# A decoder step's last four experts: where the final norm's weights are loaded, how the down weights are cut, and where the final norm stands

## The chip, the cores and the metric

The kernel runs on one core of one Trainium2 chip. The metric is the device time of one launch in microseconds (us), from several runs of the same program; beside it stands one execution that the hardware profiler recorded. TensorE (PE in the profile) does the matmuls, VectorE (DVE) and ScalarE (ACT) the elementwise work, and SyncE (SP) issues almost all transfers. All data are 32-bit floats.

## The reference

One step of a hybrid decoder layer over 320 tokens (256 prompt positions and 8 groups of 8 sampled positions), width 2048. After the mixing part and a residual add, each token goes to 2 of 32 experts, and one last norm closes the step:

```python
def _rmsnorm(x, g):
    xf = x.astype(jnp.float32)
    y = xf * lax.rsqrt(jnp.mean(xf * xf, axis=-1, keepdims=True) + NORM_EPS)
    return (y * g.astype(jnp.float32)).astype(x.dtype)
...
def expert_block(args):
    xblk, e = args
    return (jax.nn.silu(xblk @ w_gate[e]) * (xblk @ w_up[e])) @ w_down[e]
...
x = x + _hier_moe(_rmsnorm(x, norm_ffn_g), router_coarse, router_fine,
                  exp_w_gate, exp_w_up, exp_w_down)
y_prompt = _rmsnorm(hp, norm_final_g)
y_sample = _rmsnorm(hs, norm_final_g)
```

Gate and up weights of one expert are 2048 x 512, down weights 512 x 2048: 4 MB each.

## The kernel before

The program has three stages: the projections and the two head groups, the output projection with the router, and the experts. Each engine has its own instruction stream, written out by hand, and semaphores order them; nothing is scheduled by a planner. The change lies in the last part of the experts' stage, and in what follows it.

**Experts.** They are worked on four at a time (`QUAD`), in eight turns (`EQ`). Each of the four has 32 token slots (`CAP`), so four small matmuls fill the array's columns side by side; a source matmul shows as two records in the profile. If an expert gets more than 32 tokens, the whole stage is repeated in another round (`ROUNDS`); `nround` holds the number of rounds, is read by every engine after the first round, and is 1 for these inputs. A turn takes 24 pieces of weights of 2 MB (`PIECES`): pieces 0 to 15 are gate and up, 16 to 23 are down. They go into eight slots of SBUF (`NSLOT_C`, filled in the order `ESLOT`). SP asks for a piece as soon as `ex_used` says that the piece eight before it has been used; `ex_in[slot]` counts arrivals.

**The last turn** (`ex_last_quad`, and the branch `last_quad` in PE's `experts`) treats the down weights differently from the turns before: the output's 2048 columns are done in four blocks of `F` = 512 (n = 0 to 3), each in a PSUM bank of its own (`DB`: ps_C, ps_SB, ps_YB, ps_RT). Two pieces belong to a block, 16 + 2n and 17 + 2n; a piece holds two experts' columns of the block with all 512 rows. When a block's 16 matmuls (32 records, L983) are done, ACT copies the bank to `yp`, PE multiplies by the gates' transpose `gT` for the three token tiles (`combine`, L921, 6 records; tiles of 128, 128 and 64 tokens, `TT_`), and DVE adds each result to `acc` (`combined`). Every DVE and ACT operation is recorded under the line of a helper (L1286 and L1027). ACT squares and sums each part of `acc`. For blocks 0 to 2 DVE also multiplies `acc` by the final norm's weights into `og`.

**The final norm's weights** (`gfin`, spread over 128 partitions, 1 MB, into `gfb`, the place of the gathered tokens `xg`) are the last thing that SP asks for in this turn. DVE waits for them ahead of block 0's `combined`:

```python
dve.wait_ge(gfin_in, 16 * (rd + 1))
for m in range(NB):
    combined(m, True)
    if m < NB - 1:
        for t, (t0, nt) in enumerate(TT_):
            c = slice(m * F, (m + 1) * F)
            last = TT(og[0:nt, t, c], acc[0:nt, t, c], gfb[0:nt, c], ALU.mult)
```

`combine` uses two PSUM banks in turn (ps_PJ), so PE can be at most two products ahead of DVE.

**The close** stands behind the place where each engine reads `nround` and branches over the further rounds: DVE sums the squares (TENSOR_REDUCE), ACT takes the root, DVE the reciprocal, then DVE and ACT scale the rows, and SP stores them in six transfers to `o_y` (2.62 MB in all).

Of the kernel before, what the change touches and what calls it, by code (L numbers as in the profile page):

```python
# [6 lines left out]
ALU = mybir.AluOpType  # L7
# [93 lines left out]
def build_program(nc, xT, win, w_out, params, lora_mu, shT, lora_w, gmix, cst, head_cst,  # L101
# [3 lines left out]
    with ctx:  # L105
# [106 lines left out]
        over, cmx = sb(ROUNDS - 1), sb(1)  # L212
# [20 lines left out]
        og = arena[:, og_at:og_at + 9 * F].rearrange("p (t n) -> p t n", t=3)  # L233
# [109 lines left out]
        r_in, gfin_in, out_y = sem("router_in"), sem("gfin_in"), sem("out_y")  # L343
# [37 lines left out]
        def _(sp):  # L381
# [135 lines left out]
            def ex_last_quad(it):  # L517
                for c in range(PIECES):
                    sp.wait_ge(ex_used, PIECES * it + c - NSLOT_C + 1)
                    if c < 4 * QUAD:  # L520
                        ex_piece(EQ - 1, c, it)
                    else:
                        s = ESLOT[c % NSLOT_C]
                        n, e = (c - 4 * QUAD) // 2, NE - QUAD + c % 2 * 2
                        dst = arena[:, experts_at + s * BIGSLOT:experts_at + (s + 1) * BIGSLOT].rearrange("p (h k n) -> p h k n", h=2, k=4)
                        src = w_down[e:e + 2, :, n * F:(n + 1) * F].rearrange("h (k p) n -> p h k n", k=4)
                        sp.dma_start(dst, src).then_inc(ex_in[s], 16)
                sp.wait_ge(ex_used, PIECES * it + 4 * QUAD)
                sp.dma_start(gfb, gfin).then_inc(gfin_in, 16)
# [16 lines left out]
            ex_last_quad(EQ - 1)  # L546
            sp.wait_ge(named["routed"], 1)
            r = sp.value_load(nround[0:1, 0:1], min_val=1, max_val=ROUNDS)
            with sp.If(r > 1):
                with sp.Fori(1, r) as rd:  # L550
                    sp.wait_ge(named["og_done"], rd)
                    sp.nop().then_inc(sem("round_loads"), 1)
                    with sp.Fori(0, EQ - 1) as i:
                        ex_quad(i, EQ * rd + i)
                    ex_last_quad(EQ * rd + EQ - 1)
                sp.nop()
# [3 lines left out]
            def rows(t):  # L560
                t0, nt = TT_[t]
                return o_y[t0:t0 + nt, :]

            for i, t in enumerate((0, 1, 2)):
                sp.wait_ge(named["fin_done"], i + 1)
                sp.dma_start(rows(t)[:, 3 * F:], acc[0:TT_[t][1], t, 3 * F:]).then_inc(out_y, 16)
                if i == 0:
                    sp.wait_ge(named["fin_scaled"], 1)
                    sp.dma_start(rows(0)[:, 0:3 * F], og[:, 0, :]).then_inc(out_y, 16)
            sp.wait_ge(named["fin_done"], 4)  # L570
            sp.dma_start(rows(1)[:, 0:3 * F], og[:, 1, :]).then_inc(out_y, 16)
            sp.wait_ge(named["fin_scaled"], 2)
            sp.dma_start(rows(2)[:, 0:3 * F], og[0:TT_[2][1], 2, :]).then_inc(out_y, 16)
# [8 lines left out]
        def _(pe):  # L582
# [345 lines left out]
            def experts(it, opening, more, before, again, rd=None):  # L928
# [93 lines left out]
        def _(act):  # L1022
# [195 lines left out]
            def experts(it, opening, more, before, again, rd=None):  # L1218
# [9 lines left out]
                if rd is not None:  # L1228
                    for m in range(NB):
# [5 lines left out]
                    act.nop().then_inc(named["d_free"], 1)  # L1235
                    return
# [31 lines left out]

            act.nop().then_inc(named["squares_done"], 1)
            act.wait_ge(named["sum_of_squares"], 1)  # L1270
            A(rstd, ss, ACT.Sqrt, bias=eps[:, 0:1], scale=1.0 / D).then_inc(named["fin_root"], 1)
# [667 lines left out]
```

## Time and profile before

| | us |
|---|---|
| median of three runs | 2056.57 |
| lowest and highest | 2054.83, 2058.86 |
| the profiled execution | 2057.36 |
| its span, first to last instruction | 2055.6 |
| PE busy | 1678.6 (82%) |
| DVE busy | 604.0 (29%) |
| ACT busy | 280.3 (14%) |

A span is 1.8 us less than the time of the same execution. Shares of busy time are means over stages with different limits, so they don't say what the end of the program waits for. Times in the rows below count from the start of the span.

### The profile page before, as it was taken

Reading aid. Unit: us, or ns where it says so; the run is one execution under the profiler, and the core shown is the slowest. Engines: PE = TensorE matmul, PEld = TensorE weight load, DVE = VectorE, ACT = ScalarE, POOL = GpSimd, SP = SyncE. Lnnn points to the kernel's source line nnn. Section 1 sums busy time; section 2 is a strip of 40 time slices with the busy share of each in tenths; the row PEclk is TensorE's granted clock in tenths of the full one; section 3 lists DMA queues with packets and bytes.
Section 4 is the critical chain, followed back from the end, with each engine's and each line's share of the span. In section 5 each row is a group of like instructions: output and inputs, shape, how many; then the busy total and the mean of one; then the engine's idle time right before and its main releaser. Section 6 shows DMA issues by size and latency. Waiting matters only on the chain.

```text
span 2055.6 us, 25652 instructions
## 1 busy us (share of the span) xinstructions
PE 1678.6 (82%) x9134; PEld 1019.9 (50%) x9134; DVE 604.0 (29%) x1092; ACT 280.3 (14%) x559; POOL 123.9 (6%) x101
## 2 busy tenths in 40 slices
PE   8998999999999989899999577675867858576554
PEld 4776767677767767676675223132322313232111
DVE  6536263545444453631012101111110101010013
ACT  2221212222121212120012000000000000000002
POOL 0201111110202020200000000000000000000000
PEclk9999999999999999999999878887888878788777
DMA  7223222322122222316526999999999999999992
GB/s 277 98 76 111 76 89 75 110 68 97 65 91 92 74 89 75 110 49 242 216 112 290 427 427 428 428 429 429 429 428 429 429 429 429 428 429 429 428 394 103
DMA packets 71039, 510.34 MB, mean 248 GB/s; under 512 B 20400, under 2 KB 23600, under 8 KB 37584
## 3 DMA queue, kind: packets, MB, share of 16 engines
q1 hardware_dynamic: 70944, 509.60, 61.5%
q8 instruction: 29, 0.48, 0.1%
q14 instruction: 18, 0.15, 0.0%
q0 software_dynamic: 48, 0.12, 0.0%
HBM read 499.87 MB, written 9.82 MB: 248 GB/s over the span
## 4 chain that ended last, share of the span: by engine, by line
PE 52%; DMA 32%; DVE 10%; issue 2%; SPq 2%; ACT 1%; DVEq 1%; ACTq 0%
DMA arena<-w_up 21%; PE ps_PJ L626 16%; DVE arena L1286 10%; DMA arena<-w_down 10%; PE ps_C L945 8%; PE ps_PJ L824 6%; PE ps_C L684 2%; PE ps_C L707 1%; SPq L510 1%; ACT arena L1027 1%; PE ps_C L995 1%; PE ps_SB L995 1%; DMA arena<-gfin 1%; PE ps_YB L995 1%; PE ps_RT L790 1%
## 5 line engine op out<-in xcount | busy, mean ns | idle before, releaser
L626 PE MATMUL ps_PJ<-arena 128*128 128x320 f32 x1792 | 542.2, 434 | 4.0 <-ACTq L374 4.0
L945 PE MATMUL ps_C<-arena 128*32 128x512 f32 x2048 | 282.2, 714 | 179.7 <-DMA arena<-w_gate 97.3
L626 PEld LDWEIGHTS ps_PJ<-arena 128*128 128x128 f32 x1792 | 319.8, 190 | 111.5 <-issue 11.6
L945 PEld LDWEIGHTS ps_C<-arena 128*32 128x32 f32 x2048 | 80.1, 128 | 375.7 <-issue 373.5
L1286 DVE TENSOR_TENSOR arena<-arena,ps_PJ 128x512 f32<-128x512 f32 (+2 forms) x112 | 73.5, 656 | 592.3 <-PE ps_PJ L921 433.3
L1027 ACT ACTIVATE arena<-ps_C 128x512 f32<-128x512 f32 (+1 forms) x68 | 40.7, 598 | 1068.1 <-PE ps_C L945 594.6
L1286 DVE TENSOR_TENSOR arena<-arena 128x320 f32<-128x320 f32 (+12 forms) x236 | 160.0, 678 | 46.9 <-ACTq L374 26.0
L1756 POOL TENSOR_TENSOR arena<-arena 128x640 f32<-128x640 f32 (+2 forms) x80 | 118.2, 1477 | 780.6 <-DVEq L374 423.1
L824 PE MATMUL ps_PJ<-arena 128*128 128x320 f32 x512 | 145.8, 437 | 2.1 <-DVEq L374 2.1
L914 PE MATMUL ps_PJ<-arena 128*128 128x128 f32 (+1 forms) x768 | 136.2, 308 | 0.0
L914 PEld LDWEIGHTS ps_PJ<-arena 128*128 128x128 f32 (+1 forms) x768 | 104.4, 188 | 40.8 <-issue 11.7
L921 PE MATMUL ps_PJ<-arena 128*128 128x512 f32 (+1 forms) x192 | 97.1, 626 | 26.7 <-DVEq L374 23.2
L1286 DVE TENSOR_TENSOR arena<-ps_PJ,arena 128x512 f32<-128x512 f32 x32 | 22.1, 692 | 323.1 <-PE ps_PJ L914 322.9
L824 PEld LDWEIGHTS ps_PJ<-arena 128*128 128x128 f32 x512 | 95.8, 192 | 41.3 <-issue 6.4
L1027 ACT ACTIVATE arena<-arena 128x320 f32<-128x320 f32 (+11 forms) x148 | 79.7, 538 | 175.6 <-DVEq L374 89.0
L1286 DVE COPY arena<-ps_C 128x128 f32<-128x128 f32 (+2 forms) x98 | 41.6, 424 | 168.5 <-PE ps_C L716 104.8
L995 PE MATMUL ps_C<-arena 128*32 128x512 f32 x224 | 41.5, 821 | 60.6 <-DMA arena<-w_down 58.4
L921 PEld LDWEIGHTS ps_PJ<-arena 128*128 128x128 f32 (+1 forms) x192 | 26.7, 171 | 95.8 <-DVEq L374 68.5
L1286 DVE SCALAR_TENSOR_TENSOR arena<-arena 128x320 f32<-128x320 f32 (+5 forms) x146 | 68.3, 468 | 13.8 <-DVE arena L1286 8.8
L1286 DVE TENSOR_TENSOR arena<-arena,ps_C 128x512 f32<-128x512 f32 x56 | 38.6, 689 | 111.2 <-PE ps_C L707 108.9
L1027 ACT ACTIVATE arena<-ps_PJ 128x256 f32<-128x256 f32 (+2 forms) x96 | 37.0, 385 | 232.5 <-PE ps_PJ L626 142.3
L1286 DVE RECIPROCAL arena<-arena 128x320 f32<-128x320 f32 (+1 forms) x29 | 54.6, 1881 | 17.2 <-ACTq L374 14.5
(183 smaller groups left out, 1363.5 us busy)
## 6 DMA issues: line engine op xcount, KB each, us to landing
arena<-w_gate SPq DMA_DIRECT2D x64, 2048.0 KB, 20.2
arena<-w_up SPq DMA_DIRECT2D x64, 2048.0 KB, 21.0
arena<-w_down SPq DMA_DIRECT2D x64, 2048.0 KB, 21.1
arena<-win SPq DMA_DIRECT2D x59, 1024.0 KB, 4.8
arena<-w_out SPq DMA_DIRECT2D x16, 1024.0 KB, 6.7
arena<-xT SPq DMA_DIRECT2D x8, 640.0 KB, 6.9
arena<-s_ret SPq DMA_DIRECT2D x8, 512.0 KB, 3.8
o_sret<-arena SPq DMA_DIRECT2D x8, 512.0 KB, 3.8
```

The lines of the kernel that those rows point to most:

```text
L510: sp.dma_start(dst, src).then_inc(ex_in[s], 16)
L626: last = mm(pj(j)[:, 0:T], wt[j % NSLOT][:, kt, :], hT[:, kt, :], start=kt == 0, stop=kt == KT - 1)
L684: last = mm(b[:, i * P:(i + 1) * P], Lm[:, k % 2, c, :], V[:, c, :], start=True, stop=True)
L707: last = mm(bank("dv" + k)[:, c * P:(c + 1) * P], U[:, c, :], Z[:, c, :], start=True, stop=True)
L824: last = mm(pj(m)[:, 0:T], w[:, i, :], yT[:, KORD[i], :], start=i == 0, stop=i == KT - 1)
L914: last = mm(XB[b][:, k * P:(k + 1) * P], x1[0:nt, t, kt * P:(kt + 1) * P], pick[0:nt, t, :], start=t == 0, stop=t == 2)
L921: mm(XB[b][0:nt, :], gT[:, t0:t0 + nt], yp[:, n * F:(n + 1) * F], start=True, stop=True).then_inc(x_full[b], 1)
L945: last = mm((GB, UB)[u][h * CAP:(h + 1) * CAP, :], xg[:, kt, h * CAP:(h + 1) * CAP], w[h][:, k, :], start=kt == 0, stop=kt == KT - 1)
L995: last = mm(DB[n][h * CAP:(h + 1) * CAP, :], hhT[:, 2 * k + j, h * CAP:(h + 1) * CAP], w[h][:, j, n * F:(n + 1) * F], start=k + j == 0, st ...
L1027: ins = nc.scalar.activation(*args, **kw)
L1286: ins = build(*args)
L1756: ins = nc.gpsimd.tensor_tensor(*args)
```

## The change

There are three parts.

1. SP asks for `gfin` behind piece 19, in front of pieces 20 to 23, and DVE waits for it behind block 0's `combined`.
2. A piece of down weights of the last turn now holds half the rows of all four experts (`e` is the half), where it held all rows of two. PE waits for a block's second piece in the middle of the block.
3. The close stands inside the round, in front of the reading of `nround`. ACT does a square root of one element that nobody reads (`unread`) behind the transposed gates' copy; the last block's product with the weights is split off for two tiles, and rows are scaled and stored in other pieces.

```diff
@@ -521,12 +521,38 @@
                         ex_piece(EQ - 1, c, it)
...
-                        n, e = (c - 4 * QUAD) // 2, NE - QUAD + c % 2 * 2
-                        dst = arena[:, experts_at + s * BIGSLOT:experts_at + (s + 1) * BIGSLOT].rearrange("p (h k n) -> p h k n", h=2, k=4)
-                        src = w_down[e:e + 2, :, n * F:(n + 1) * F].rearrange("h (k p) n -> p h k n", k=4)
+                        n, e = (c - 4 * QUAD) // 2, c % 2
+                        dst = arena[:, experts_at + s * BIGSLOT:experts_at + (s + 1) * BIGSLOT].rearrange("p (h k n) -> p h k n", h=4, k=2)
+                        src = w_down[NE - QUAD:NE, :, n * F:(n + 1) * F].rearrange("h (k e p) n -> e p h k n", k=2, e=2)[e, :, :, :, :]
                         sp.dma_start(dst, src).then_inc(ex_in[s], 16)
-                sp.wait_ge(ex_used, PIECES * it + 4 * QUAD)
-                sp.dma_start(gfb, gfin).then_inc(gfin_in, 16)
+                    if c == 4 * QUAD + 3:
+                        sp.wait_ge(ex_used, PIECES * it + 4 * QUAD)
+                        sp.dma_start(gfb, gfin).then_inc(gfin_in, 16)
...
+                sp.wait_ge(named["fin_done"], 4 * rd + 1)
+                sp.nop().then_inc(sem("stores_begun"), 1)
+                sp.dma_start(rows(0, 0, 2 * F), og[:, 0, 0:2 * F]).then_inc(stored, 16)
+                sp.wait_ge(named["fin_scaled"], 2 * rd + 1)
+                sp.nop().then_inc(sem("stores_begun"), 1)
+                sp.dma_start(rows(1, 2 * F, D), og[:, 1, 2 * F:]).then_inc(stored, 16)
...
+            store_rows(0, out_y)
             sp.wait_ge(named["routed"], 1)
             r = sp.value_load(nround[0:1, 0:1], min_val=1, max_val=ROUNDS)
...
-            def rows(t):
-                t0, nt = TT_[t]
-                return o_y[t0:t0 + nt, :]
-
-            for i, t in enumerate((0, 1, 2)):
-                sp.wait_ge(named["fin_done"], i + 1)
-                sp.dma_start(rows(t)[:, 3 * F:], acc[0:TT_[t][1], t, 3 * F:]).then_inc(out_y, 16)
-                if i == 0:
-                    sp.wait_ge(named["fin_scaled"], 1)
-                    sp.dma_start(rows(0)[:, 0:3 * F], og[:, 0, :]).then_inc(out_y, 16)
-            sp.wait_ge(named["fin_done"], 4)
-            sp.dma_start(rows(1)[:, 0:3 * F], og[:, 1, :]).then_inc(out_y, 16)
-            sp.wait_ge(named["fin_scaled"], 2)
-            sp.dma_start(rows(2)[:, 0:3 * F], og[0:TT_[2][1], 2, :]).then_inc(out_y, 16)
...
                 if last_quad:
                     pe.wait_ge(named["gT_done"], it + 1)
                     for n in range(NB):
-                        w = [piece_in(4 * QUAD + 2 * n + e, it).rearrange("p (h k n) -> p h k n", h=2, k=4) for e in range(2)]
                         for k in range(4):
+                            if k % 2 == 0:
+                                w = piece_in(4 * QUAD + 2 * n + k // 2, it).rearrange("p (h k n) -> p h k n", h=4, k=2)
                             for h in range(QUAD):
-                                last = mm(DB[n][h * CAP:(h + 1) * CAP, :], hhT[:, k, h * CAP:(h + 1) * CAP], w[h // 2][:, h % 2, k, :],
+                                last = mm(DB[n][h * CAP:(h + 1) * CAP, :], hhT[:, 2 * (k % 2) + k // 2, h * CAP:(h + 1) * CAP], w[:, h, k % 2, :],
                                           start=k == 0, stop=k == 3)
-                                if k == 3 and h % 2 == 1:
-                                    last.then_inc(ex_used, 1)
+                            if k % 2 == 1:
+                                last.then_inc(ex_used, 1)
                         pe.wait_ge(named["yp_part"], NB * rd + n + 1)
                         combine(n)
...
                 if rd is not None:
+                    A(unread, eps[:, 0:1], ACT.Sqrt)
                     for m in range(NB):
                         act.wait_ge(ex_used, PIECES * it + 4 * QUAD + 2 * m + 2)
                         A(yp[:, m * F:(m + 1) * F], DB[m][:, :], ACT.Copy).then_inc(named["yp_part"], 1)
...
+                    act.nop().then_inc(named["squares_done"], 1)
+                    act.wait_ge(named["sum_of_squares"], rd + 1)
+                    A(rfin, ss, ACT.Sqrt, bias=eps[:, 0:1], scale=1.0 / D).then_inc(named["fin_root"], 1)
+                    act.wait_ge(named["acc_done"], rd + 1)
+                    A(og[:, 1, 2 * F:], og[:, 1, 2 * F:], ACT.Copy, scale=rfin[:, 1:2]).then_inc(named["fin_scaled"], 1)
+                    nt = TT_[2][1]
+                    A(og[0:nt, 2, 0:3 * F], og[0:nt, 2, 0:3 * F], ACT.Copy, scale=rfin[0:nt, 2:3]).then_inc(named["fin_scaled"], 1)
...
-                dve.wait_ge(gfin_in, 16 * (rd + 1))
-                for m in range(NB):
+
+                def gained(m, t):
+                    nt = TT_[t][1]
+                    c = slice(m * F, (m + 1) * F)
+                    TT(og[0:nt, t, c], acc[0:nt, t, c], gfb[0:nt, c], ALU.mult)
+
+                for m in range(NB - 1):
                     combined(m, True)
-                    if m < NB - 1:
-                        for t, (t0, nt) in enumerate(TT_):
-                            c = slice(m * F, (m + 1) * F)
-                            last = TT(og[0:nt, t, c], acc[0:nt, t, c], gfb[0:nt, c], ALU.mult)
-                last.then_inc(named["og_done"], 1)
+                    if m == 0:
+                        dve.wait_ge(gfin_in, 16 * (rd + 1))
+                    for t in range(3):
+                        gained(m, t)
+                combined(NB - 1, True)
+                gained(NB - 1, 0)
+                dve.wait_ge(named["squares_done"], rd + 1)
+                RED(ss, ss4[:, :, :], AX_X, ALU.add).then_inc(named["sum_of_squares"], 1)
+                gained(NB - 1, 1)
+                dve.wait_ge(named["fin_root"], rd + 1)
+                RECIP(rfin, rfin).then_inc(named["acc_done"], 1)
+                TSC(og[:, 0, 0:2 * F], og[:, 0, 0:2 * F], rfin[:, 0:1], None, ALU.mult).then_inc(named["fin_done"], 1)
+                TSC(og[:, 0, 2 * F:], og[:, 0, 2 * F:], rfin[:, 0:1], None, ALU.mult).then_inc(named["fin_done"], 1)
+                TSC(og[:, 1, 0:2 * F], og[:, 1, 0:2 * F], rfin[:, 1:2], None, ALU.mult).then_inc(named["fin_done"], 1)
+                nt = TT_[2][1]
+                STT(og[0:nt, 2, 3 * F:], acc[0:nt, 2, 3 * F:], rfin[0:nt, 2:3], gfb[0:nt, 3 * F:], ALU.mult, ALU.mult).then_inc(named["fin_done"], 1)
...
-            dve.wait_ge(named["squares_done"], 1)
-            RED(ss, ss4[:, :, :], AX_X, ALU.add).then_inc(named["sum_of_squares"], 1)
-            dve.wait_ge(named["fin_root"], 1)
-            RECIP(rstd, rstd).then_inc(named["acc_done"], 1)
-            for t, (t0, nt) in enumerate(TT_):
-                a_ = acc[0:nt, t, 3 * F:]
-                STT(a_, a_, rstd[0:nt, t:t + 1], gfb[0:nt, 3 * F:], ALU.mult, ALU.mult).then_inc(named["fin_done"], 1)
-            TSC(og[:, 1, :], og[:, 1, :], rstd[:, 1:2], None, ALU.mult).then_inc(named["fin_done"], 1)
```

What is left out: the other four stores are written like the two that stand (tile 0 columns 1024 on behind `fin_done` 2, tile 1 columns 0 to 1024 behind `fin_done` 3, tile 2 columns 1536 on behind `fin_done` 4, tile 2 columns 0 to 1536 behind `fin_scaled` 2), `og` grows from 4608 to 6144 words, the old close on ACT is taken out like the one on DVE, and further rounds, which do not happen here, get the same treatment.

On SP's queue, the end of the first round, from the last turn's gate and up pieces on. First before, then changed:

```order
L510 DMA arena<-w_gate 128x4096 x4
L510 DMA arena<-w_up 128x4096 x4
L527 DMA arena<-w_down 128x8x512 x8
L529 DMA arena<-gfin 128x2048
L548 TENSOR_LOAD nround
L548 ISA x2
L549 COMPARE_AND_BRANCH
```

```order
L527 DMA arena<-w_down 128x8x512 x4
L530 DMA arena<-gfin 128x2048
L527 DMA arena<-w_down 128x8x512 x4
L540 DMA o_y<-arena 128x1024
L543 DMA o_y<-arena 128x1024
L546 DMA o_y<-arena 128x1024
L549 DMA o_y<-arena 128x1024
L552 DMA o_y<-arena 64x512
L555 DMA o_y<-arena 64x1536
L575 TENSOR_LOAD nround
```

The weights' transfer has moved past four pieces, and the stores past the reading of `nround` and its branch.

On PE, block 3 of the last turn with the semaphores that its first instructions wait for (the rows of the other blocks are alike). First before, then changed:

```order
L983 MATMUL ps_RT<-arena 32x512 [waits expert_in3,expert_in2]
L983 MATMUL ps_RT<-arena 32x512 x15
L921 MATMUL ps_PJ<-arena 128x512 [waits x_free1,yp_part]
L921 MATMUL ps_PJ<-arena 128x512 [waits x_free0]
L921 MATMUL ps_PJ<-arena 64x512 [waits x_free1]
```

```order
L999 MATMUL ps_RT<-arena 32x512 [waits expert_in2]
L999 MATMUL ps_RT<-arena 32x512 x7
L999 MATMUL ps_RT<-arena 32x512 [waits expert_in3]
L999 MATMUL ps_RT<-arena 32x512 x7
L936 MATMUL ps_PJ<-arena 128x512 [waits x_free1,yp_part]
```

The number of matmuls is the same; the wait for the second piece has moved eight matmuls back.

On DVE, from block 3's sums to the scaled rows. Before, the first three rows stand at the end of the round, and the others behind the code of the further rounds:

```order
L1286 TENSOR_TENSOR arena<-arena,ps_PJ 128x512 x2
L1286 TENSOR_TENSOR arena<-arena,ps_PJ 64x512
L1732 TENSOR_LOAD nround
...
L1733 UNCONDITIONAL_BRANCH
L1737 UNCONDITIONAL_BRANCH
L1286 TENSOR_REDUCE arena<-arena 128x3
L1289 ISA
L1286 RECIPROCAL arena<-arena 128x3
```

```order
L1302 TENSOR_TENSOR arena<-arena,ps_PJ 128x512 x2
L1302 TENSOR_TENSOR arena<-arena,ps_PJ 64x512
L1302 TENSOR_TENSOR arena<-arena 128x512
L1302 TENSOR_REDUCE arena<-arena 128x3
L1302 TENSOR_TENSOR arena<-arena 128x512
L1302 RECIPROCAL arena<-arena 128x3
L1302 TENSOR_SCALAR arena<-arena 128x1024 x3
L1302 SCALAR_TENSOR_TENSOR arena<-arena 64x512
L1764 TENSOR_LOAD nround
```

Between the last sum and the reduction the load and the branches are gone and one product has come in; a second stands between the reduction and the reciprocal.

## Rows read from the trace of the kernel before

**Rows 1.** Part 2 of the page: transfers' busy share in tenths, 40 slices.

```profile
DMA  7223222322122222316526999999999999999992
```

**Rows 2.** Busy time in stretches: PE, PEld, DVE, ACT, POOL; granted clock, DMA share, GB/s.

```profile
1940.00:1962.00 22.00, 14.09 (x75) 4.03 (x75) 2.74 (x4) 0.00 (x0) 0.00 (x0) 0.72 1.01 429
1966.00:2010.00 44.00, 18.94 (x107) 6.10 (x107) 1.80 (x3) 2.23 (x4) 0.00 (x0) 0.66 1.05 387
2047.00:2055.00 8.00, 0.00 (x0) 0.00 (x0) 1.76 (x2) 1.40 (x1) 0.00 (x0) 0.50 0.95 323
```

**Rows 3.** SP's issues of pieces 20 and 23; below each its time to landing.

```profile
1977.16 2.77 SPq L527 DMA_DIRECT2D arena<-w_down  x1
...
arena<-w_down SPq DMA_DIRECT2D x1, 2048.0 KB, 17.5
...
1991.31 5.29 SPq L527 DMA_DIRECT2D arena<-w_down  x1
...
arena<-w_down SPq DMA_DIRECT2D x1, 2048.0 KB, 19.5
```

**Rows 4.** The chain that ended last, from 1980 on: start, us, what.

```profile
1982.64 5.54 PE ps_C L983 x32
...
1996.65 16.61 DMA arena<-gfin
...
2013.29 0.70 DVE arena L1286
```

**Rows 5.** Timeline of PE, 1976 to 2042: start, us, operation, idle before.

```profile
1980.01 1.11 PE L966 MATMUL ps_PJ<-arena 128*128 128x128 f32 x4 [2.86 <-DVEq L374]
...
1988.90 1.98 PE L921 MATMUL ps_PJ<-arena 128*128 128x512 f32 x4 [0.78 <-ACTq L374]
...
2014.09 1.97 PE L921 MATMUL ps_PJ<-arena 128*64 128x512 f32 x2 [23.20 <-DVEq L374]
...
2028.54 3.11 PE L921 MATMUL ps_PJ<-arena 128*128 128x512 f32 x6 [0.85 <-ACTq L374]
2031.58 3.64 PE L983 MATMUL ps_RT<-arena 128*32 128x512 f32 x32
2036.07 3.11 PE L921 MATMUL ps_PJ<-arena 128*128 128x512 f32 x6 [0.85 <-ACTq L374]
```

**Rows 6.** Timeline of all engines, 2013 to 2056.

```profile
2032.62 2.14 DVE L1286 TENSOR_TENSOR arena<-arena 128x512 f32<-128x512 f32 x3 [0.25 <-DVE arena L1286]
...
2035.38 0.60 ACT L1027 ACTIVATE arena<-ps_RT 128x512 f32<-128x512 f32 x1 [2.03 <-PE ps_RT L983]
...
2040.68 0.19 ACT L1027 ACTIVATION_READ_ACCUMULATOR arena<-arena 64x1 f32 x1
2042.31 1.28 ACT L1027 ACT_TABLE_LOAD   x1 [1.44 <-issue]
2044.23 0.17 DVE L1286 TENSOR_REDUCE arena<-arena 128x3 f32<-128x12 f32 x1 [4.33 <-issue]
...
2044.87 0.18 DVE L1286 RECIPROCAL arena<-arena 128x3 f32<-128x3 f32 x1 [0.47 <-ACTq L374]
...
2046.04 0.37 SPq L566 DMA_DIRECT2D o_y<-arena  x1
...
2047.90 1.02 DVE L1286 TENSOR_SCALAR arena<-arena 128x1536 f32<-128x1536 f32 x1
```

**Rows 7.** Transfers from 2040 to 2044.5 by kind.

```profile
q8 instruction: 2, 0.03, 3.3%
q14 instruction: 2, 0.02, 1.4%
```

**Rows 8.** Stretches as in rows 2: around the first and the second restart of PE.

```profile
1976.90:1980.00 3.10, 0.25 (x4) 0.00 (x0) 1.80 (x3) 0.60 (x1) 0.00 (x0) 0.93 1.05 386
...
1983.00:1986.40 3.40, 3.40 (x20) 0.92 (x16) 0.00 (x0) 0.00 (x0) 0.00 (x0) 0.50 1.05 387
...
2017.00:2041.00 24.00, 19.46 (x114) 5.12 (x106) 12.36 (x18) 9.03 (x23) 0.00 (x0) 1.00 0.01 2
```

More of the change, by code:

```diff
@@ L211, in build_program @@
         oh1, oh2 = (sb(3 * EG).rearrange("p (t n) -> p t n", t=3) for _ in range(2))
-        over, cmx = sb(ROUNDS - 1), sb(1)
+        over, cmx, unread, rfin = sb(ROUNDS - 1), sb(1), sb(1), sb(3)
         assert place[0] <= top[0], (place[0], top[0])
@@ L232, in build_program @@
         og_at = experts_at + ESLOT[0] * BIGSLOT
-        og = arena[:, og_at:og_at + 9 * F].rearrange("p (t n) -> p t n", t=3)
+        og = arena[:, og_at:og_at + 3 * D].rearrange("p (t n) -> p t n", t=3)
         SETUP = [(0, 2), (2, 2), (4, 4), (8, 4), (12, 4)]
@@ L342, in build_program @@
         x_in, x1T_done, tr_full, tr_free = [sem(f"x_in{i}") for i in range(4)], sem("x1T_done"), sem("transposed"), sem("x1_done")
-        r_in, gfin_in, out_y = sem("router_in"), sem("gfin_in"), sem("out_y")
+        r_in, gfin_in, out_y, out_more = sem("router_in"), sem("gfin_in"), sem("out_y"), sem("out_more")
         x_full, x_free = [sem("x_full0"), sem("x_full1")], [sem("x_free0"), sem("x_free1")]
@@ new lines, in rows, with store_rows @@
+            def rows(t, a, b):
+                t0, nt = TT_[t]
+                return o_y[t0:t0 + nt, a:b]
+            def store_rows(rd, stored):
+                sp.wait_ge(named["fin_done"], 4 * rd + 1)
[4 more added lines that the diff above has]
+                sp.dma_start(rows(1, 2 * F, D), og[:, 1, 2 * F:]).then_inc(stored, 16)
+                sp.wait_ge(named["fin_done"], 4 * rd + 2)
+                sp.nop().then_inc(sem("stores_begun"), 1)
+                sp.dma_start(rows(0, 2 * F, D), og[:, 0, 2 * F:]).then_inc(stored, 16)
+                sp.wait_ge(named["fin_done"], 4 * rd + 3)
+                sp.nop().then_inc(sem("stores_begun"), 1)
+                sp.dma_start(rows(1, 0, 2 * F), og[:, 1, 0:2 * F]).then_inc(stored, 16)
+                sp.wait_ge(named["fin_done"], 4 * rd + 4)
+                sp.nop().then_inc(sem("stores_begun"), 1)
+                sp.dma_start(rows(2, 3 * F, D), og[0:NS * TS, 2, 3 * F:]).then_inc(stored, 16)
+                sp.wait_ge(named["fin_scaled"], 2 * rd + 2)
+                sp.nop().then_inc(sem("stores_begun"), 1)
+                sp.dma_start(rows(2, 0, 3 * F), og[0:NS * TS, 2, 0:3 * F]).then_inc(stored, 16)
@@ L550, in _ @@
                 with sp.Fori(1, r) as rd:
-                    sp.wait_ge(named["og_done"], rd)
-                    sp.nop().then_inc(sem("round_loads"), 1)
+                    sp.wait_ge(out_y, 96)
                     with sp.Fori(0, EQ - 1) as i:
@@ L555, in _ @@
                     ex_last_quad(EQ * rd + EQ - 1)
+                    store_rows(rd, out_more)
+                    sp.wait_ge(out_more, 96 * rd)
+                    sp.nop().then_inc(sem("stores_begun"), 1)
                 sp.nop()
@@ L1267, in _ @@
             n[0], n[1] = base + per * r, 0
-            act.nop().then_inc(named["squares_done"], 1)
-            act.wait_ge(named["sum_of_squares"], 1)
-            A(rstd, ss, ACT.Sqrt, bias=eps[:, 0:1], scale=1.0 / D).then_inc(named["fin_root"], 1)
-            act.wait_ge(named["acc_done"], 1)
-            for t in (0, 2):
-                nt = TT_[t][1]
-                A(og[0:nt, t, :], og[0:nt, t, :], ACT.Copy, scale=rstd[0:nt, t:t + 1]).then_inc(named["fin_scaled"], 1)
         @block.vector
```

## The prediction

> **What bounds the kernel now.** I read the page's slices first. From the 21st slice on the transfers are busy nine tenths or more in every slice but the last [rows 1]: the experts' stage is set by the weights' stream, and PE, granted 0.72 of its full clock, waits for it. The stretches give the rate: 429 GB/s for gate and up pieces, 387 GB/s for the last turn's down pieces, which are cut into runs of 2 KB [rows 2]. So a 2 MB down piece (2,097,152 bytes) takes 5.4 us, a block's two pieces 10.8 us, and gfin's 1 MB about 2.4 us. No transfer in this stage is removed or added, so the stream ends when it ended. What can change is how much work stands behind its end.
>
> Then the chain. Block 0's matmuls run from 1982.64, and then nothing until gfin lands: 1996.65 + 16.61 = 2013.26, and DVE's first sum starts at 2013.29 [rows 4]. The last down piece had landed at 1991.31 + 19.5 = 2010.8 [rows 3]. PE had made block 0's first two products at 1988.90 (4 records) and then stood for 23.2 us, since DVE had freed neither bank [rows 5]. So almost four blocks' sums, three blocks' matmuls, the close and the stores all lie behind the stream: 2055.6 - 2013.3 = 42.3 us. I make the sum against the span of 2055.6; the same execution's time is 2057.36, the median of the runs 2056.57, and I take the gain in the span off the median.
>
> **Parts 1 and 2: gfin earlier, pieces by halves of the rows.** Up to piece 19 nothing changes. SP now waits for all 16 gate and up pieces before gfin, where piece 20 needed 13; these four are released within the last four matmuls of one group, so that wait ends together with the old one, at 1977.16 [rows 3]. The queue runs 17.5 to 19.5 us ahead of the landing [rows 3], so the longer issue of 5.3 us starves nothing. Pieces 20 to 23 land 2.4 us later each: 20 at 1977.16 + 17.5 + 2.4 = 1997.1, then one per 5.4 us at 2002.5, 2007.9 and 2013.3. gfin lands 2.4 us behind piece 19, which lands 5.4 before 1994.7: at 1991.7.
>
> Block 0 is summed when its products come. At the full clock, 3.04 us lie between a block's first product and the next block's matmuls (2028.54 to 2031.58) and 4.49 us between those and the block's own first product (2031.58 to 2036.07) [rows 5]. From 1988.90: block 1's matmuls start at 1991.9, after its pieces; block 2's at 1999.5, waiting from 2001.3 to 2002.5 for piece 21; its products start at 2005.2, block 3's matmuls at 2008.2, after piece 22. Half of them are done at 2010.1, and PE waits 3.2 us for piece 23. DVE's gfin wait sits behind the first three sums, past 1991.7: hidden; if gfin came later, 4 us are free before block 1's sums need DVE.
>
> What stays behind the last piece, at the full clock:
> - half a block's matmuls: 3.64 / 2 = 1.8 us, and 0.85 through ACT's copy to the first product (2035.22 to 2036.07) [rows 5, 6];
> - from the first product to the end of the last square's readout: 2036.07 to 2040.87, 4.8 us [rows 5, 6].
>
> That puts the last square's end at 2013.3 + 7.5 = 2020.8.
>
> **Part 3: the close in the round.** Before, the reduction started at 2044.23, 3.36 us after that square, with nothing in front of it but the load of `nround` and the branches (4.33 us idle, "issue"); four instruction fetches run in that stretch [rows 6, 7]. That goes. In its place come two products of 128x512, 2.14 / 3 = 0.71 us each with 0.25 between operations [rows 6]. The first stands beside the last square and is hidden. The second stands between the reduction and the reciprocal. I allow 0.1 us from the square to the reduction, then 0.17 + 0.25 + 0.71 + 0.2 = 1.35 to the reciprocal, where it was 0.64. The table load of 1.28 us [rows 6], hidden behind DVE's stall before, would stand on this path now, but the root that nobody reads takes it to about 1982.4, before ACT's first copy, which waits for matmuls until 1988; without that cover it would cost about 1.3. The reciprocal starts at 2020.8 + 1.45 = 2022.25, where it was 2044.87.
>
> The stores: before, the first was issued 1.17 us behind the reciprocal's start, and the span ended at +10.7; the stream of 2.62 MB was the limit, 323 GB/s at a busy share of 0.95 [rows 2, 6]. Now the first store is ready after one 128x1024 scaling (1.02 x 1024 / 1536 = 0.68 us [rows 6]), at +1.1, but with 512 KB where there were 256. ACT's two scalings lie beside DVE's. Bounds: +10.7 at the same rate, +9.4 if 2.62 MB move at 387 GB/s (6.8 us, not 8.1). I take +10.3, since the last transfer is still the one of 64 rows that used few runs. End: 2032.55.
>
> **The clock.** After 2.86 us without a matmul (up to 1980.01) the granted clock was 0.5, still so at 1986.4 though PE was back at work; while blocks followed each other with 0.85 us gaps it stayed at 1.0, from 2017 to 2041 [rows 5, 8]. The new wait for piece 23 is 3.2 us, so I expect the lower level (1.2 GHz) right where the rest of the path begins. The half block then takes 3.6, not 1.8; a product's two records took 1.97 at that level (2014.09) against about 1.1 [rows 5], which adds up to 2.2 over three products if the level lasts through them. So 1.5 to 4.0; I take 2.5, since the lower level lasted 2.9 us of work in one case (2014.09 to 2017) and at least 6.4 in the other (1980.01 to 1986.4). Gain: 2055.6 - 2035.05 = 20.5 us; 2056.57 - 20.5 = **2036.1**.
>
> The Trainium skill, TensorE: Matmul & The Clock Gate, section "HAM oscillation — how this bites in real kernels", says that bursts shorter than the wait for the next load are each run at the lower clock. The 2.86 us case agrees. It speaks against cutting a block in two around a wait: by the page the sum is 2036.1, and without its rule 2033.5, the first rival.
>
> **The rivals.**
> - *The clock holds over the last wait.* For it: the wait is shorter than most of those that lowered the clock, and any earlier delay of a block fills it. Then 2056.57 - 23.0 = 2033.5.
> - *PE, not the stream, paces the blocks.* At the lower level throughout, matmuls take 7.3, and the products up to 5.6 with 0.85 before them: 13.7 a block, against 10.8 of stream. Block 3 would start at 2019.4 and the reciprocal at 2036.5: span 2046.8, time 2047.8. Against it: the work from 1988.9 on is nearly continuous and such work held 1.0 [rows 8]. Half way, one block at the lower level, costs up to 2 us beyond 2033.5, since block 3 has 3.2 us to spare.
> - *SP ends last.* SP now reads `nround` and branches behind its last store, at about +4.9 (DVE's last scaling ends near +3.8, then two issues of 0.4 to 0.6 us); DVE's same passage took 4.33 us [rows 6]. That gives +9.2, hidden below +10.3; if the fetches queue behind the stores, up to 4 us more: 2037 to 2040. The Trainium skill, Runtime: NRT & Kernel Launch, section "Instruction fetch mechanics", says a taken branch out of the loaded pages stalls on a fetch; rows 7 agree.
> - *Slower than before: the new pieces read slowly.* A piece now takes rows of four experts instead of two. If the eight pieces went at 263 GB/s instead of 387, they would take 63.8 us instead of 43.4 and eat the 20.5. Below that rate it decides. Going from large runs to 2 KB runs cost only a tenth [rows 2], and runs and their number stay as they are. At 340 GB/s the time would be 2042.
> - *The order does not do what it says:* gfin, though asked for earlier, lands with the last piece. Then the blocks stand as before, and what is left is the stall of 3.4 less the product of 0.7, and 0.4 in the stores: 2053.5. Against it: landings kept the order of asking.
>
> **How the numbers follow.** The clock falls: 0.56. It holds: 0.2. PE paces, in part or whole (2037 to 2048): 0.08. SP ends last: 0.05. Pieces slower but still a gain (2038 to 2052): 0.06. gfin late: 0.01. No change from something unforeseen: 0.01. Slower than before: 0.03. So faster 0.95, the same 0.02, slower 0.03. A difference of 0.2% (4.1 us) is what a measurement of this kernel can tell. The first two cases, with stores +9.4 to +10.7 and a clock cost up to 4.0, span 2032.6 to 2038; to hold 8 in 10 with part of the others I give 2032.5 to 2041.
>
> **What would show it.** gfin lands near 1991.7 and the last down piece near 2013.3; DVE sums block 0 from 1990 on; PE stands some 3 us in the middle of block 3's matmuls, and the second half takes 3.6 us at a clock of 0.5; no "issue" wait in front of the reduction, and no table load there; reciprocal between 2022 and 2026, the end 9.4 to 10.7 us later. Wrong would make it: down pieces below 387 GB/s; a block whose matmuls start later than its second piece lands; an end that SP reaches well after the last store has landed.

## The result, and the profile after

The changed kernel takes 2036.76 us (median of four runs, 2034.52 to 2037.36), the kernel before in the same comparison 2056.41: ratio 0.9905, 95% interval 0.9892 to 0.9917. That is 19.7 us less; 20.5 were forecast. The profiled execution took 2036.68 us, with a span of 2034.9.

First SP's timeline in the changed kernel, as in [rows 3]: its issue of gfin (start, us) and of the four last pieces.

```profile
1975.49 2.27 SPq L530 DMA_DIRECT2D arena<-gfin  x1
1977.81 19.19 SPq L527 DMA_DIRECT2D arena<-w_down  x4
```

The same kernel's transfers, with the time from issue to landing at the end, which answers to [rows 4]:

```profile
arena<-gfin SPq DMA_DIRECT2D x1, 1024.0 KB, 14.2
```

gfin lands at 1975.5 + 14.2 = 1989.7. Then PE's timeline, which answers to [rows 5] (start, us, operation, records, idle before and who ended it).

```profile
1987.21 3.03 PE L936 MATMUL ps_PJ<-arena 128*128 128x512 f32 x6 [0.82 <-ACTq L374]
1990.18 3.64 PE L999 MATMUL ps_SB<-arena 128*32 128x512 f32 x32
...
2000.59 1.92 PE L999 MATMUL ps_YB<-arena 128*32 128x512 f32 x16 [0.98 <-DMA arena<-w_down]
...
2006.38 1.92 PE L999 MATMUL ps_RT<-arena 128*32 128x512 f32 x16
2011.22 2.94 PE L999 MATMUL ps_RT<-arena 128*32 128x512 f32 x16 [2.92 <-DMA arena<-w_down]
2014.96 4.83 PE L936 MATMUL ps_PJ<-arena 128*128 128x512 f32 x6 [0.80 <-ACTq L374]
```

Block 0's six product records run through at 1987.21, where PE stood for 23.2 us before; all that is left behind the last piece is half of block 3, which waited 2.92 us. That half took 2.94 us against 1.92 for the first, and the products 4.83 against 3.11 [rows 5]. The stretches say why (columns as in rows 2; the granted clock is the third number from the end):

```profile
2006.40:2012.00 5.60, 2.68 (x25) 0.68 (x28) 2.74 (x4) 1.45 (x4) 0.00 (x0) 1.00 0.47 176
2012.00:2018.80 6.80, 6.00 (x17) 1.51 (x10) 0.71 (x2) 1.32 (x3) 0.00 (x0) 0.50 0.00 0
```

PE ran at 2.4 GHz up to 2012.0 and at 1.2 GHz for the next 6.8 us. Next the changed kernel's timeline of the close, as in [rows 6]:

```profile
2021.30 0.19 ACT L1043 ACTIVATION_READ_ACCUMULATOR arena<-arena 64x1 f32 x1
2021.71 0.17 DVE L1302 TENSOR_REDUCE arena<-arena 128x3 f32<-128x12 f32 x1 [0.26 <-ACTq L1253]
...
2022.03 0.69 DVE L1302 TENSOR_TENSOR arena<-arena 128x512 f32<-128x512 f32 x1 [0.15 <-DVE arena L1302]
2022.75 0.18 DVE L1302 RECIPROCAL arena<-arena 128x3 f32<-128x3 f32 x1
...
2024.01 0.35 SPq L540 DMA_DIRECT2D o_y<-arena  x1
...
2028.29 1.21 SPq L555 DMA_DIRECT2D o_y<-arena  x1
```

SP's own instructions behind the stores, by source line (L575 loads `nround`, L576 branches, L592 holds the first instructions behind the branch, L105 is the end of the program; count, ns min/median/max, first and last start):

```profile
L575 SPq TENSOR_LOAD <-nround x1: 1577/1577/1577, 2029.5 to 2029.5; - x1
...
L576 SPq COMPARE_BRANCH  x1: 50/50/50, 2031.5 to 2031.5; - x1
...
L592 SPq EVENT_SEMAPHORE  x2: 17/22/28, 2034.3 to 2034.4; - x2
...
L105 SPq COMPARE_BRANCH  x1: 41/41/41, 2034.5 to 2034.5; - x1
```

And the last store among the transfers, with its time to landing:

```profile
o_y<-arena SPq DMA_DIRECT2D x1, 384.0 KB, 4.8
```

The "issue" wait of 4.33 us in front of the reduction is gone. But the last store, issued at 2028.29, landed 4.8 us later, at 2033.1, and SP got from its branch at 2031.5 to the end's first instruction only at 2034.5: the program ends 1.8 us behind the last landing. Before, that was 0.4 us (2049.75 + 5.4 = 2055.15, end 2055.58).

### The profile page after: what moved, and what is told of

Its sections match the earlier page's. It is cut to its first block, busy times and chain, and to the rows that moved or that the text cites. A ratio compares the mean times of both kernels' runs of the same rounds, so it can differ in the third digit from the quotient of the medians.

```text
span 2034.9 us, 25650 instructions
## 1 busy us (share of the span) xinstructions
PE 1682.4 (83%) x9134; PEld 1020.5 (50%) x9134; DVE 605.2 (30%) x1094; ACT 279.8 (14%) x560; POOL 124.0 (6%) x101
## 4 chain that ended last, share of the span: by engine, by line
PE 52%; DMA 32%; DVE 10%; issue 2%; SPq 1%; ACT 1%; DVEq 1%; ACTq 0%
DMA arena<-w_up 21%; PE ps_PJ L641 16%; DMA arena<-w_down 11%; DVE arena L1302 10%; PE ps_C L960 8%; PE ps_PJ L839 7%; PE ps_C L699 2%; PE ps_C L722 1%; SPq L510 1%; ACT arena L1043 1%; PE ps_C L1011 1%; PE ps_SB L1011 1%; PE ps_YB L1011 1%; PE ps_RT L805 1%; PE ps_SB L756 1%
## 5 line engine op out<-in xcount | busy, mean ns | idle before, releaser
L1302 DVE SCALAR_TENSOR_TENSOR arena<-arena 128x320 f32<-128x320 f32 (+4 forms) x144 | 66.8, 464 | 13.5 <-DVE arena L1302 8.7
## 6 DMA issues: line engine op xcount, KB each, us to landing
arena<-w_up SPq DMA_DIRECT2D x64, 2048.0 KB, 20.9
arena<-w_down SPq DMA_DIRECT2D x64, 2048.0 KB, 20.8
```

Of the source, the lines that this page charges most:

```text
L1302: ins = build(*args)
```

## The experiments

Executions differ by some 2 us either way before the part that changed is reached: PE got the last down piece at 2011.2 here and between 2009.4 and 2013.4 over the ten profiles with gfin early. In the kernel before, that piece landed at 2010.8, with gfin 2.4 behind it. So besides ratios I read each profile from the point where PE (or DVE) gets what it last waited for to the end of the span. I call it the **tail**. "Second half" and "products" are the last block's 16 records behind the wait and its six product records.

| kernel | last wait ends, us | tail, us | second half | products | time (median), us | ratio (95%) |
|---|---|---|---|---|---|---|
| before | 2013.29 (gfin) | 42.3 | | 3.11 | | 1 |
| changed | 2011.22 | 23.7 | 2.94 | 4.83 | 2036.76 | 0.9905 (0.9892 to 0.9917) |
| part 1 | 2009.40 | 23.9 | | 3.11 | 2036.85 | 0.9911 (0.9894 to 0.9927) |
| parts 1, 2 | 2011.15 | 22.0 | 1.92 | 3.11 | 2036.55 | 0.9909 (0.9893 to 0.9926) |
| part 2 | 2011.9 (gfin) | 42.5 | | 3.11 | 2055.77 | 1.0001 (0.9992 to 1.0011) |
| part 3 | 2011.4 (gfin) | 42.0 | | 3.11 | 2055.33 | 0.9995 (0.9986 to 1.0005) |
| parts 1, 3 | 2011.72 | 22.9 | | 3.11 | 2036.41 | 0.9905 (0.9888 to 0.9921) |

**Part 1 alone.**

```diff
+                    if c == 4 * QUAD + 3:
+                        sp.wait_ge(ex_used, PIECES * it + 4 * QUAD)
+                        sp.dma_start(gfb, gfin).then_inc(gfin_in, 16)
-                sp.wait_ge(ex_used, PIECES * it + 4 * QUAD)
-                sp.dma_start(gfb, gfin).then_inc(gfin_in, 16)
...
-                dve.wait_ge(gfin_in, 16 * (rd + 1))
                 for m in range(NB):
                     combined(m, True)
+                    if m == 0:
+                        dve.wait_ge(gfin_in, 16 * (rd + 1))
```

> The kernel before with part 1 alone: gfin asked for behind piece 19, DVE's wait for it behind block 0's sums; pieces and close as before. Theory A (the time is what stands behind the last down piece): three blocks' matmuls and the first three blocks' sums move under the stream, a whole block 3 (3.6 us, with the lower clock up to 6), its sums, the stall of 3.4 us and the close stay: about 15.5 us less than before, 2041 us. Rival B (most of the gain comes from the close, the landing order hardly counts): at most 4 us less, 2052 or more.

Measured 2036.85 us: as far as the times can tell, this part by itself is the whole gain. Rival B is out. Theory A's direction holds, but it took this version 4.2 us too slow. Part of the reason is in this kernel's PE timeline:

```profile
1998.84 6.26 PE L984 MATMUL ps_YB<-arena 128*32 128x512 f32 x32 [5.07 <-DMA arena<-w_down]
2005.95 3.11 PE L922 MATMUL ps_PJ<-arena 128*128 128x512 f32 x6 [0.84 <-ACTq L374]
2009.40 3.64 PE L984 MATMUL ps_RT<-arena 128*32 128x512 f32 x32 [0.34 <-DMA arena<-w_down]
```

With whole pieces PE waits 5.07 us for block 2, whose matmuls then run slowly (6.26 us), and that leaves only 0.34 us to wait before block 3, which runs at the full clock. The lower level was paid where there was time for it. The expectation had put it on block 3, at up to 2.4 us (6 for 3.6); where the rest of the 4.2 comes from is not shown. The tail is what the rows of the kernel before give at the full clock: from block 3's first matmul to its end it has 24.0 us (2031.58 to 2055.58), and here it is 23.9.

**Parts 1 and 2.** The edit is part 1's and the pieces' from the diff of the change.

> The kernel before with parts 1 and 2: gfin early and pieces by halves of the rows, the close as before. Theory A: half of block 3's matmuls move in front of the last landing, 1.8 us at the full clock and up to 3.6 at the lower one, less than with part 1 alone: 2038 to 2039.5 us. Rival C (the wait inside the block lowers the clock, which eats what the halves bring): equal to part 1 alone within 0.5 us.

The times don't tell it from part 1 (2036.55 against 2036.85, intervals overlap). The tails do: 22.0 against 23.9. PE waited 2.87 us inside block 3 and yet the clock held, so the half took 1.92. Theory A's 1.8 is measured at 1.9 in the tail for the case that the clock holds, but its 2038 to 2039.5 us was 1.5 to 3 us too slow, since it rests on the expectation for part 1. Rival C describes the other case, as the changed kernel's own profile shows.

**Part 2 alone.**

> The kernel before with part 2 alone: pieces by halves, gfin still last. Theory A: all pieces have landed when gfin does, so nothing changes: within 1 us of before, and the down stretch still moves 387 GB/s. Rival D (pieces that read from four experts are read at another rate): a rate other than 387 GB/s in that stretch, and the time moves by the stretch's difference.

Ratio 1.0001. The down stretch moves what it moved before [rows 2]; the stretch in this kernel:

```profile
1965.00:2008.00 43.00, 16.59 (x107) 5.13 (x107) 1.80 (x3) 2.23 (x4) 0.00 (x0) 0.75 1.05 388
```

388 GB/s against 387: how many experts a piece reads from makes no difference, and rival D is out.

**Part 3 alone.**

> The changed kernel with gfin last and its wait ahead of block 0's sums, and the old pieces: part 3 alone. Theory A: the stall of 3.4 us goes, a product of 0.7 stays in front of the reciprocal, and the stores with SP's load and branch behind them end 12.1 us behind it where it was 10.7, as in the changed kernel's trace: about 1.5 us less than before, 2055 us. Rival B: the close brings most of the 20 us: below 2045 us.

Ratio 0.9995, tail 42.0 against 42.3. The reduction came 0.2 us behind the last square instead of 3.4, the reciprocal 1.04 behind that instead of 0.64, and the end 12.05 behind the reciprocal (2041.40 to 2053.45) instead of 10.7. That is 1.4 us won, and in this execution block 1's matmuls took 5.30 us at the lower clock where they took 4.17 before, which hides 1.1 of it. From part 1 to parts 1 and 3 the tail shrinks by 1.0. The times show none of this: part 3 alone has an interval that includes 1, and the intervals of part 1 and of parts 1 and 3 overlap.

**Parts 1 and 3** (the changed kernel with whole pieces).

> The changed kernel with the old pieces (all rows of two experts): parts 1 and 3. Measured so far: part 1 alone has 24.1 us from the last down piece's landing to the end, with block 3 whole and at the full clock since PE waits only 0.3 us for it. Theory A: the halves take 1.9 us of matmuls off the path but put a wait of 2.9 us inside the block that lowers the clock; without them the path is 1.7 longer and the clock holds: from the landing to the end 23 to 24 us, within 1 us of the changed kernel (23.7). Rival: 1.8 to 2 us slower than the changed kernel.

Tail 22.9, time 2036.41: nothing is lost without the halves. In the changed kernel's profile they took 1.7 us of matmuls off the tail and put 2.7 back through the clock.

**gfin asked for last, DVE's wait still behind block 0's sums.**

```diff
-                    if c == 4 * QUAD + 3:
-                        sp.wait_ge(ex_used, PIECES * it + 4 * QUAD)
-                        sp.dma_start(gfb, gfin).then_inc(gfin_in, 16)
+                sp.wait_ge(ex_used, PIECES * it + 4 * QUAD)
+                sp.dma_start(gfb, gfin).then_inc(gfin_in, 16)
```

> The changed kernel with gfin asked for last again; DVE's wait stays behind block 0's sums. Theory A (the transfer's place counts, through DVE's sums and PE's two banks): block 1's sums wait for gfin, so one block less than before stands behind it: some 7.5 us less than with the close alone, 2047 us. Rival (the wait's place in DVE's stream is what counts): as fast as the changed kernel plus the 2.4 us of transfer, 2039 us.

2049.43 us, ratio 0.9967 (0.9955 to 0.998). PE is one block further when it stops. Its timeline in this kernel, and DVE's first work behind gfin:

```profile
1993.11 1.98 PE L935 MATMUL ps_PJ<-arena 128*128 128x512 f32 x4 [0.82 <-ACTq L374]
...
2011.32 2.14 DVE L1301 TENSOR_TENSOR arena<-arena 128x512 f32<-128x512 f32 x3 [21.88 <-DMA arena<-gfin]
...
2014.29 1.97 PE L935 MATMUL ps_PJ<-arena 128*64 128x512 f32 x2 [19.19 <-DVEq L374]
2016.19 5.76 PE L998 MATMUL ps_YB<-arena 128*32 128x512 f32 x32
```

So the chain runs through DVE's in-order stream and PE's two banks, and the place of the transfer counts; the rival's 2039 us is out. It is 2.4 us slower than expected. The tail is 37.2 us (2011.32 to 2048.5), 4.8 less than with the close alone, not 7.5. The expectation had left out that DVE, once gfin is there, first does block 0's three products (2.14 us) and only then the sum that frees PE's bank: PE restarts 3.0 us behind gfin, where it was 0.8 with the close alone. That is 2.2 of the 2.7 us. The rest is block 2's matmuls at the lower clock, 5.76 us, where the block behind gfin took 5.30 with the close alone.

**gfin early, DVE's wait in its old place.**

```diff
+                dve.wait_ge(gfin_in, 16 * (rd + 1))
                 for m in range(NB - 1):
                     combined(m, True)
-                    if m == 0:
-                        dve.wait_ge(gfin_in, 16 * (rd + 1))
```

> The changed kernel with DVE's wait for gfin in its old place, ahead of block 0's sums; gfin is still asked for early. Theory A: gfin lands 1.3 us behind block 0's first product, that delay fits into the waits for pieces 21 and 23, and nothing is left of it at the end: as the changed kernel within 0.5 us. Rival (the place of the wait matters): 1 us or more slower.

2034.22 us, ratio 0.9898 (0.9882 to 0.9915), tail 20.8. PE stood 0.88 us for block 0's third product, and nothing of it reached the end; moving DVE's wait brought nothing by itself. The tail is 2.9 us below the changed kernel's, which is what the lower clock cost there (2.7), since here the clock held over a wait of 2.63 us. Nothing more can be read from it.

**No square root that nobody reads.**

```diff
-                    A(unread, eps[:, 0:1], ACT.Sqrt)
```

> The changed kernel without the square root that nobody reads. The table load of 1.28 us then stands in front of ACT's root, behind the last square. Theory A: the root starts about 0.9 us later, of which the product beside it hides some: reciprocal 0.5 to 0.8 us later relative to the last square. Rival: 1.3 us later, the whole load.

The timeline of ACT and DVE in this kernel:

```profile
2022.09 0.19 ACT L1043 ACTIVATION_READ_ACCUMULATOR arena<-arena 64x1 f32 x1
2022.44 1.28 ACT L1043 ACT_TABLE_LOAD   x1 [0.17 <-ACT arena L1043]
...
2024.18 0.18 DVE L1301 RECIPROCAL arena<-arena 128x3 f32<-128x3 f32 x1 [0.68 <-ACTq L374]
```

From the last square's readout to the reciprocal 1.90 us (2022.28 to 2024.18) instead of 1.26 (2021.49 to 2022.75): 0.64, as theory A had it. The times can't show that: 2032.81 us, ratio 0.9887 (0.9871 to 0.9904), over runs from 2032.64 to 2038.17.

**SP's load of `nround` ahead of the stores**, the branch still behind them.

```diff
-            store_rows(0, out_y)
             sp.wait_ge(named["routed"], 1)
             r = sp.value_load(nround[0:1, 0:1], min_val=1, max_val=ROUNDS)
+            store_rows(0, out_y)
```

> The changed kernel with SP's load of nround in front of the stores' waits; the branch still stands behind them. Theory A (SP's load of 1.6 us and its branch of 2.8 us end the program, 1.2 us behind the last store's landing): the load's 1.6 us go from SP's path, and the end is set by the last store: 1.2 to 1.4 us less than the changed kernel. Rival (the last store's landing sets the end anyway): no difference.

Theory A fell. 2036.09 us, ratio 0.9902 (0.9885 to 0.9918), and what follows the branch did not start earlier, by SP's instructions in this kernel:

```profile
L576 SPq COMPARE_BRANCH  x1: 50/50/50, 2029.6 to 2029.6; - x1
...
L592 SPq EVENT_SEMAPHORE  x2: 17/22/28, 2034.2 to 2034.3; - x2
...
L105 SPq COMPARE_BRANCH  x1: 41/41/41, 2034.4 to 2034.4; - x1
```

It is 4.6 us from the branch to the instructions behind it (L592), where the changed kernel has 2.8, and 4.8 to the end's first instruction, where that has 3.0; SP ends at about the same distance behind the stores. What it waits for is not its own work, and it isn't the landing either: in the next run, whose branch comes first, L592 starts 3.4 us before the end's first instruction.

**Branch first.** Load and branch ahead of the stores, which then stand in both arms.

```diff
-            store_rows(0, out_y)
             sp.wait_ge(named["routed"], 1)
             r = sp.value_load(nround[0:1, 0:1], min_val=1, max_val=ROUNDS)
             with sp.If(r > 1):
+                store_rows(0, out_y)
...
             with sp.Else():
-                sp.nop()
+                store_rows(0, out_y)
```

> The changed kernel with SP's load of nround and its branch ahead of the stores, which stand in both arms. In the trace with the load alone moved, the branch took 4.6 us instead of 2.8 and ended at the same distance from the last store. Theory E (the branch's instruction fetches wait behind the stores' data in the same transfer engines): with the branch done before the first store, the program ends 0.4 us behind the last landing, as before: 1.0 to 1.3 us less than the changed kernel. Rival (something else at the end takes this time): no difference.

The same instructions in this kernel, where the branch is L575:

```profile
L575 SPq COMPARE_BRANCH  x1: 50/50/50, 1998.2 to 1998.2; - x1
...
L592 SPq EVENT_SEMAPHORE  x2: 17/22/28, 2029.9 to 2029.9; - x2
...
L105 SPq COMPARE_BRANCH  x1: 41/41/41, 2033.3 to 2033.3; - x1
```

From the reciprocal (2023.07) to the end (2033.7) it is 10.6 us, where the changed kernel has 12.15: 1.5 less, a little more than theory E's 1.0 to 1.3. In times 2034.54 us, ratio 0.9894 (0.9878 to 0.9911); the interval overlaps the changed kernel's.

**Matmuls in the last wait.** `GB` is a bank that is free by then.

```diff
                         for k in range(4):
+                            if n == NB - 1 and k == 2:
+                                for _ in range(8):
+                                    mm(GB[:, 0:P], ident, ones, start=True, stop=True)
```

> The changed kernel with eight 128x128 matmuls, whose result nobody reads, between the halves of block 3, into a bank that is free. Theory A (the idle 2.9 us lower the clock, and the half block and the three products behind it run at 1.2 GHz): the clock stays at 1.0, the half block takes 1.9 us instead of 2.9 and the products 3.8 from the first start to the last sum instead of 5.6: 2 to 3 us less than the changed kernel. Rival (the clock falls for another reason, or the matmuls last past the landing): no gain or a loss.

PE's timeline in this kernel:

```profile
2008.36 2.05 PE L998 MATMUL ps_C<-arena 128*128 128x128 f32 x16
2011.36 1.93 PE L1002 MATMUL ps_RT<-arena 128*32 128x512 f32 x16 [0.94 <-DMA arena<-w_down]
2014.10 3.11 PE L936 MATMUL ps_PJ<-arena 128*128 128x512 f32 x6 [0.82 <-ACTq L374]
```

And the stretch behind it, columns as in rows 2:

```profile
2014.00:2020.00 6.00, 3.06 (x6) 0.87 (x6) 3.47 (x6) 2.47 (x8) 0.00 (x0) 1.00 0.01 3
```

The clock stays at 1.0, the half takes 1.93 and the products 3.11: tail 20.9 against 23.7, 2.8 us less. Time 2034.22 us, ratio 0.9893 (0.9876 to 0.9909). One rival stands: that the clock would have held here without these matmuls, as it did in two of the six profiles with an unfilled wait (the kernel with DVE's wait in its old place has the same median and a tail of 20.8). It held in both profiles with the matmuls, here and in the next run, which by luck alone would happen in 1 of 9 cases (an estimate from two in six). So the gain is likely, and not proven.

**Both together.**

> The last one with the eight matmuls between the halves of block 3 as well. If both act apart: from the last down piece's landing to the end 20.95 - 1.3 = 19.6 us, where the changed kernel has 23.7; some 4 us less than the changed kernel, 2033 us or less. Rival (one hides the other): no better than the eight matmuls alone.

Tail 19.8 (2011.66 to 2031.5), 3.9 us below the changed kernel; 2033.02 us, ratio 0.9886 (0.987 to 0.9903). The two act apart: 2.8 us for the clock and 1.1 for the branch, which is 0.4 less than it brought alone. It beats the kernel before clearly, and the changed kernel by 3.7 us in the medians, though the two intervals still overlap.

## Why the prediction was right

**Part 1, the core of the sum, held.** The stream's end stayed what the tail hangs on: gfin landed at 1989.7 (forecast 1991.7, in an execution that ran 2 us ahead), the four blocks' work moved under the pieces, and PE stood 2.92 us (forecast 3.2) in the middle of block 3. Part 1 alone and its two halves (the transfer's place, DVE's wait) show that the transfer's place is the cause: 18.4 us of tail. With gfin early, the place of DVE's wait made no difference.

**The sum of the tail.** Forecast 21.75 us, measured 23.7:
- half block, copy, products and squares with the clock: 9.95 forecast (1.8 + 0.85 + 4.8 + 2.5), 10.27 measured (2011.22 to 2021.49). The clock's 2.5 was 2.74 (2.94 - 1.92, and 4.83 - 3.11).
- square to reduction 0.1, measured 0.22; reduction to reciprocal 1.35, measured 1.04, since the product starts 0.15 us behind the small reduction.
- reciprocal to end 10.3 (bounds 9.4 and 10.7), measured 12.15. **This is the term that was mis-sized.** 0.45 of the 1.85 is a last landing at +10.35, not +9.9: the first store was issued 1.26 us behind the reciprocal, not 1.1, and the new cut of the stores brought nothing (+10.3 before). The other 1.4 is SP, which ends last with its load and branch. The prediction had named this as a rival at 0.05, with SP from +4.9 to +9.2 and so hidden, and up to 4 us more "if the fetches queue behind the stores". What made it come true was mostly a size: SP had issued its last store only at +6.75 (2029.50), since the last three issues took 1.1 to 1.2 us each and not 0.4 to 0.6. Load and branch then took 4.8 us up to L592, against the 4.33 that were read from DVE beside idle transfers. A wait of the branch behind the stores shows clearly only in the run with the load moved, where it took 4.6 us and not 2.8. The Trainium skill, Runtime: NRT & Kernel Launch, section "Instruction fetch mechanics", gives the stall on a taken branch; what it costs beside stores is from these runs.

The total came right in part by luck. The prediction's end of the stream, 2013.3, was built on a profile that ran late (DVE got gfin at 2013.3, and at 2011.3 to 2011.9 in the three other profiles with gfin last). In the changed kernel's profile it came at 2011.2, which offset the 1.95 us in the sum of the tail, and over the ten profiles with gfin early it came at 2011.4 on average. By the tails the change is worth 18.6 us and not 20.5, by the medians 19.7; there the forecast was 0.7 us too low.

**Where the account was too generous.** The prediction gave parts 2 and 3 terms of their own. Part 2 is worth 1.9 us only when the clock holds over the wait that it creates. Over six profiles with that wait (2.63 to 2.92 us) the cost was 2.7 and 2.8 (changed, branch first), 1.4 and 1.3 (no unread root, load first) and none (parts 1 and 2, wait ahead). So the mean cost is 1.4, and it eats most of the 1.7 to 1.9. The forecast's 0.56 for a fall was fair; its 2.5 for the cost is near the upper end. The case that it had read its rule from, the 2.86 us up to 1980.01 [rows 5], was a wait for DVE and not for a load. Part 3 is worth about 1 us of tail, and about 2.4 with the branch ahead of the stores (an estimate: 1.0 and 1.4). The times resolve neither part: parts 1 and 2, parts 1 and 3 and all three have medians within 0.4 us.

**The other rivals.** PE did not pace the end: in every run with gfin early it stood waiting for the last piece. Pieces did not read slowly (388 GB/s). gfin was not late.

## What to carry to other kernels

When a stage is paced by a stream of transfers, count what stands behind its last byte, and look for a small transfer at the end of the queue whose wait sits ahead of an in-order engine: 1 MB cost 18 us here, not its own 2.4. Work that is cut finer to shorten such a tail can lose what it brings, since PE's clock can fall in the wait that it opens; filling that wait seems to help. And a branch that was free while an engine waited can be on the path once it stands behind the last stores: look at when the engine is through with issuing them.

## What the runs showed of the hardware

- A branch of SP behind the stores took 3.0 us to the end's first instruction, and 4.8 when it stood 1.9 us earlier: it ended 1.4 and 1.2 us behind the last store's landing. The packets that the transfer engines moved, by kind (number, MB, share of the engines): in the changed kernel from 2032.4 to 2034.4; in the one with the load moved, whose branch stands at 2029.6, from 2030.8 to 2032.3 and from 2032.3 to 2034.3; and in the one with the branch first from 2031.2 to 2033.3.

```profile
q14 instruction: 2, 0.02, 2.1%
...
q1 hardware_dynamic: 58, 0.32, 96.1%
...
q14 instruction: 2, 0.02, 2.0%
...
q1 hardware_dynamic: 71, 0.31, 68.4%
```

The two instruction packets came only when the stores' data (q1) were nearly through, whether the branch stood at 2031.5 or at 2029.6, and the kernel with the branch first has none there. That fits fetches of the earlier branch that wait for the stores' data. Data do not hold up every fetch, though: two other instruction packets ran between 2029.9 and 2030.8 in the changed kernel, among the stores' data, and in the changed kernel the branch's 2.8 us may be no more than it takes on idle engines. No run holds the packets apart from the data, so this stays an inference.

- The same wait of 2.6 to 2.9 us lowered PE's clock in four of six executions, for a cost between 1.3 and 2.8 us. The Trainium skill, TensorE: Matmul & The Clock Gate, section "HAM oscillation — how this bites in real kernels", describes work between loads that is shorter than the wait for the next load, and there each such piece of work starts at the lower clock. Here the half block ahead of the wait took 1.92 us, and the clock fell in four cases and held in two. Ahead of block 2, with parts 1 and 2, it also held over 3.20 us; with whole pieces it fell over 4.33 and 5.07 us. So the length of the wait alone does not decide.
- SP's issue of a store took 0.35 us for the first and 1.2 for the last, which moves less data (the rows above); before, the longest was 0.76 us. The growth isn't steady: in seven other profiles of this order of stores the second took 1.1 to 1.4 us and the third 0.4, but the last two took 1.1 to 1.25 in all. What sets it is not shown.
